# Statistics of 20 RMSNorm tiles: squares summed on GpSimd before one matmul, and weight casts on four DMA chains

## The reference

```python
def rmsnorm(x, g):
    x32 = x.astype(jnp.float32)
    y = x32 * lax.rsqrt(jnp.mean(x32 * x32, axis=-1, keepdims=True) + NORM_EPS)
    return y.astype(x.dtype) * g

u = modulate(rmsnorm(h, ffn1_norm[l]), sh1, sc1)
h = h + 0.5 * g1 * swiglu(u, ffn1_w_gate[l], ffn1_w_up[l], ffn1_w_down[l])
u = modulate(rmsnorm(h, mix_norm[l]), sh2, sc2)
h = h + g2 * hybrid_mixer(u, ...)
u = modulate(rmsnorm(h, ffn2_norm[l]), sh3, sc3)
h = h + 0.5 * g3 * swiglu(u, ffn2_w_gate[l], ffn2_w_up[l], ffn2_w_down[l])
return rmsnorm(h, final_norm)
```

## Time and profile before

| | us |
|---|---|
| median of 3 runs | 3066.21 |
| lowest and highest run | 3059.49, 3182.67 |
| the profiled execution's own time | 3062.68 |
| span of its slowest core, core 0 | 3061.1 |
| spans of the eight cores | 3041.2 to 3061.1 |
| mean granted PE clock of the cores | 0.983 to 0.985 |
| PE busy, share of the span | 2843.8, 93% |
| DVE busy | 1402.7, 46% |
| ACT busy | 1255.3, 41% |
| POOL busy (nearly all of it the issue of DMAs) | 75.1, 2% |

### The profile page before, as it was taken

The page is one execution under the profiler, slowest core; times in us unless marked ns, Lnnn a source line. Parts: engine busy times, 40 slices in busy tenths (PEclk is TensorE's granted clock), DMA queues, the critical chain, the costliest instruction groups (busy, mean ns, idle before and its releaser), DMA issues.

```text
span 3061.1 us, 42691 instructions; the slowest of 8 cores (3041.2 to 3061.1 us)
## 1 busy us (share of the span) xinstructions
PE 2843.8 (93%) x16528; PEld 1355.0 (44%) x16528; DVE 1402.7 (46%) x2808; ACT 1255.3 (41%) x1751; POOL 75.1 (2%) x147
## 2 busy tenths in 40 slices
PE   3999988999899999999978999999999999999998
PEld 1344433444454444544434445544454444444443
DVE  2555215445465445344445545654535444532532
ACT  2421105335434456454235453555755624322311
POOL 1000000000000000000000000000000000000000
PEclk9999999999999999999989999999999999999999
DMA  9678985476924934552793334334245368436446
GB/s 212 116 146 160 201 217 170 125 213 129 205 81 111 180 124 99 121 155 104 234 281 117 97 104 125 111 116 144 75 135 154 119 234 281 138 110 200 165 121 223
DMA packets 144138, 470.76 MB, mean 154 GB/s; under 512 B 17376, under 2 KB 21216, under 8 KB 129760
## 3 DMA queue, kind: packets, MB, share of 16 engines
q1 hardware_dynamic: 127600, 399.80, 41.2%
q0 software_dynamic: 16336, 68.23, 15.0%
HBM read 452.83 MB, written 100.66 MB: 181 GB/s over the span
## 4 chain that ended last, share of the span: by engine, by line
PE 75%; DMA 12%; ACT 5%; DVE 5%; SPq 1%; issue 1%; POOL 0%; ACTq 0%; DVEq 0%; POOLq 0%
PE psall L127 75%; ACT pt L127 3%; DMA hst<-xL 2%; DMA h<-hst 2%; DMA h<-qk 2%; DMA wf<-sdn 2%; SPq L127 1%; DMA wf<-wgu 1%; DMA wf<-w_ada 1%; ACT mu L127 1%; DMA qk<-h 1%; ACT L127 1%; DVE accsb L127 1%; DVE qk L127 1%; DVE mu L127 1%
## 5 line engine op out<-in xcount | busy, mean ns | idle before, releaser
L127 PE MATMUL psall<-uf,wf 128*128 128x512 bf16 x4224 | 1036.7, 384 | 39.7 <-DMA wf<-wgu 13.2
L127 ACT ACTIVATE pt<-psall 128x1024 bf16<-128x1024 f32 (+3 forms) x520 | 452.8, 872 | 458.4 <-PE psall L127 456.9
L127 PEld LDWEIGHTS psall<-uf,wf 128*128 128x128 bf16 x4224 | 399.9, 99 | 472.2 <-issue 36.7
L127 PE MATMUL psall<-actf,wf 128*128 128x512 bf16 x2112 | 514.4, 385 | 16.6 <-DMA wf<-sdn 16.6
L127 ACT ACTIVATE ftf<-psall 128x512 f32<-128x512 f32 x352 | 210.0, 597 | 658.3 <-PE psall L127 638.4
L127 DVE SCALAR_TENSOR_TENSOR ftf<-ftf,psall 128x512 f32<-128x512 f32 x352 | 241.1, 685 | 443.6 <-ACT ftf L127 412.5
L127 PE MATMUL psall<-mu,wm 128*128 128x512 bf16 (+2 forms) x1312 | 328.9, 381 | 13.7 <-ACT mu L127 9.6
L127 PE MATMUL psall<-mixb,wf 128*128 128x512 bf16 x1408 | 323.0, 384 | 9.0 <-ACT mixb L127 6.7
L127 PEld LDWEIGHTS psall<-actf,wf 128*128 128x128 bf16 x2112 | 200.0, 99 | 226.0 <-issue 18.7
L127 DVE SCALAR_TENSOR_TENSOR hst<-psall,SC,hst 128x512 f32<-128x512 f32 x120 | 90.0, 750 | 434.5 <-PE psall L127 260.4
L127 DVE TENSOR_TENSOR actf<-ftf,psall 128x512 bf16<-128x512 f32 x264 | 180.9, 685 | 195.2 <-PE psall L127 192.8
(11 more groups left out here) (113 smaller groups left out, 1993.6 us busy)
## 6 DMA issues: line engine op xcount, KB each, us to landing
wf<-sgu SPq DMA_DIRECT2D x242, 512.0 KB, 4.1
wf<-sdn SPq DMA_DIRECT2D x192, 352.0 KB, 4.2
h<-hst SPq DMA_DIRECT2D x120, 256.0 KB, 4.5
xt<-h SPq DMA_DIRECT2D x30, 1024.0 KB, 7.2
wm<-w_ada POOLq DMA_DIRECT2D x32, 512.0 KB, 11.0
hst<-xL SPq DMA_DIRECT2D x64, 256.0 KB, 7.4
qk<-h SPq DMA_DIRECT2D x16, 1024.0 KB, 6.6
h<-qk SPq DMA_DIRECT2D x16, 1024.0 KB, 9.6
```

The source lines that it names most:

```text
L127: ins = getattr(eng, o.fn[0])(**o.fn[1])
```

## The change

`pooled_stats` is new. It squares the eight pieces on ACT as before, but sums the squares on POOL: the first two into the float32 tile that later holds the reciprocal root (`rsf0`), the next ones onto it, and the last sum is written as bfloat16 into the buffer of the last square. Two empty steps follow, and then one matmul with the ones matrix. The PSUM bank is taken after that and not before. It applies to norms with the tag "XT" and a source and to `final_gen`; all other norms keep `square_stats`. The squares are still bfloat16. The casts of the FFN2 weights go round four resources and four semaphores instead of two.

```diff
+        def pooled_stats(pcs, sqr, acc, accR, out):
+
+            first = None
+            for k, (ap, res) in enumerate(pcs):
+                sq = square(ap, res, sqr)
+                if k == 0:
+                    first = sq
+                elif k == 1:
+                    I("pool", "tensor_tensor", r=[first[1], sq[1]], w=[accR], out=acc[:], in0=first[0][:], in1=sq[0][:], op=ALU.add)
+                elif k < len(pcs) - 1:
+                    I("pool", "tensor_tensor", r=[accR, sq[1]], w=[accR], out=acc[:], in0=acc[:], in1=sq[0][:], op=ALU.add)
+                else:
+                    I("pool", "tensor_tensor", r=[accR, sq[1]], w=[sq[1]], out=sq[0][:], in0=acc[:], in1=sq[0][:], op=ALU.add)
+                    out.append(sq)
+                yield
+            yield
+            yield
...
@@ norm_gen
+            rt, rtR = rs
+            total = []
+            if tag == "XT" and src is not None:
+                for _ in pooled_stats(pcs, sqr, rt, rtR, total):
+                    yield 1
             while not banks.free:
                 yield None
             bank = banks.take()
-            for _ in square_stats(pcs, sqr, bank, split):
-                yield 1
-            rt, rtR = rs
+            if total:
+                stat_mm(bank, total[0], 0, 1)
+            else:
+                for _ in square_stats(pcs, sqr, bank, split):
+                    yield 1
             rstd(bank, D, rt, rtR)
...
@@ final_gen
+            rt, rtR = rsF.next()
+            total = []
+            for _ in pooled_stats(XTP, btF, rt, rtR, total):
+                yield 1
             while not psF.free:
                 yield None
             bank = psF.take()
-            for _ in square_stats(XTP, btF, bank):
-                yield 1
-            rt, rtR = rsF.next()
+            stat_mm(bank, total[0], 0, 1)
             rstd(bank, D, rt, rtR)
...
-        convR = [Res("conv0"), Res("conv1")]
+        convR = [Res(f"conv{i}") for i in range(4)]
...
-                i = len(conv) % 2
+                i = len(conv) % 4
```

## The result

| | before | after |
|---|---|---|
| median, us | 3065.68 (8 runs) | 3083.27 (8 runs) |
| lowest and highest run | 3059.49, 3349.96 | 3078.97, 3094.76 |
| the profiled execution's own time | 3062.68 | 3082.51 |
| spans of the eight cores | 3041.2 to 3061.1 | 3058.1 to 3081.0 |
| mean granted PE clock of the cores | 0.983 to 0.985 | 0.975 to 0.979 |

The ratio is 1.007 (95% interval 1.0054 to 1.0087): within 2%, but slower by more than the measurement is uncertain.

What follows compares the result with a forecast made beforehand. PE's matmul count was taken as the bound, at the end and nearly so elsewhere. 3062.7 − 15.1 + 24.2 − 14.1 − 5 + 1 = 3053.7, plus 3.5 from profiled execution to median, gives 3057 us; range 3030 to 3092.

Steps and rivals of the forecast that it cites:

- all of it path: Ten dense tiles: 70 matmuls fewer at 0.216 us each shorten the kernel by their full 15.1 us.
- Add and pace: POOL's 140 new adds: 1.24 us each, one every 1.32 us with the gap between dependent adds.
- Quick adds: Rival, chance 0.18: POOL adds take 0.69 us, dense stall is 3.0 us instead of 24.2, time 3035 us.
- slow adds: Rival, chance 0.17: slower POOL adds lengthen PE's dense waits; at 2.0 us an add, stall 69 us and time 3102 us.
- Dense stall: Ten dense tiles: PE waits at the one matmul for the seventh add, 24.2 us in all, against 15.1 us saved.
- Costing it at nothing: Dense tiles: three square buffers hold ACT 6.5 us behind POOL's adds, counted as no loss of time.
- an add of 1.32 us keeps up, and the stall is 0 in all ten: Ten mixed tiles: steps lie 3 to 4 us apart, so PE never waits for adds; 14.1 us of matmuls gained.
- if the mixed stretches do not shorten: Sign named beforehand that the forecast is wrong: stretches where mixer and FFN interleave get no shorter.
- locks: Rival, chance 0.05: POOL and DVE exclude each other, 17 us of DVE delay in mixed stretches, time 3074 us.
- 5 us gained of the 9.5: FFN2 casts held back by adds: PE waits near 424 and 806 us shrink by 5 us, range 0 to 9.5.
- bursts of casts: Rival, chance 0.08: four casts at once delay weight loads at three places by some 5 us each, time 3077 us.
- The four chains themselves I cost at nothing: FFN2 casts on four chains instead of two: no cost, since the longest cast wait is 20.9 us.

Runs made afterwards that it cites:

- e5: The kernel after without POOL adds and without seven of eight squares, casts on two chains; ratio to the kernel before 0.994.
- e3: The kernel after with the one matmul five steps later in dense tiles; ratio to the kernel before 0.9995.
- e9: e6 with Ln of a pooled tile waiting only for the matmul, no longer for POOL as well; ratio to the kernel before 0.9913.
- e6: e3 with each FFN2 cast also waiting for the last PE instruction written before it (paced casts); ratio to the kernel before 0.9936.
- e14: e9 with the two mixed tiles at 1512 and 2157 us left on eight matmuls; ratio to the kernel before 0.9857, median 3021.59 us.
- e7: The kernel before with paced FFN2 casts and nothing else; ratio to the kernel before 0.9933.
- e11: e6 with every POOL add replaced by a memset of the same tile with the same waits; one run, 3069.86 us.
- e10: The kernel before with the casts on four chains and nothing else; ratio to the kernel before 1.0083.
- e1: The kernel after with only the ten dense tiles pooled, four chains of casts; ratio to the kernel before 1.0088.
- e2: The kernel after with only the ten mixed tiles pooled, four chains of casts; ratio to the kernel before 1.0014.
- e13: The kernel after with the casts on two chains as before; ratio to the kernel before 1.0036.

## Why the prediction was wrong

**Matmuls: count and pitch right, "all of it path" not quite.** 140 fewer, 0.216 us each. e5 gets 10.9 of 12.1 us from eight mixed tiles, e3 11.0 and e9 12.1 of the 15.1 from the ten dense ones. The 3 to 4 us that are missing in the dense stretches may have come out in the rest of the kernel, which gives 7.5 us in e3; that is not shown.

**Add and pace: right.** 1.30 us for 1.32. *Quick adds* and *slow adds* are both out.

**Dense stall: the wait about right, a term left out.** Forecast +9.1 us net, measured +20.8. PE's waits for POOL are 30.1 us as a mean over the cores (28.2 to 32.2). In order of the tiles they are 2.9, 10.6, 4.1, 0, 2.8, 2.2, 0, 2.8, 2.2 and 2.4 us, where the forecast had 2.2, 2.0, 3.8, 1.2, 2.9, 2.5, 1.2, 2.9, 2.5 and 3.0. The 10.6 us are not the adds alone. The seven adds take 8.9 us here, and they could not begin earlier, because the squares of this tile wait for its load (after, core 4):

```profile
346.98 1.67 ACT L127 ACTIVATE btf<-xt 128x512 bf16<-128x512 f32 x3 [22.97 <-DMA xt<-xL]
```

In this stretch PE waits 6.4 us before as well, for DVE and ACT, and 5.4 us in e3, so only about 5 of the 10.6 are new. That leaves about 25 us of new wait for the 24.2 of the forecast. The agreement of the sums is in part luck, since two tiles without a wait make up for the one with more. The step that failed in the dense tiles is that the sum ended with the wait: it had no term for the 1.2 GHz level behind it, 7 to 9 us. With the about 4 us of matmuls above, that is the 11.7 us between +9.1 and +20.8.

ACT, held by the three buffers, waits 14.7 us for POOL in the dense tiles (mean over the cores), where the prediction read 6.5. Costing it at nothing was right all the same: in e5 no add holds ACT, and its dense tiles gain no more than those of e3 (8.1 us against 11.0).

**Mixed tiles: the step that failed.** The prediction said "an add of 1.32 us keeps up, and the stall is 0 in all ten". Keep up it does, and PE never waits for POOL there; but a stall of 0 was read as a gain of 14.1, and in nine tiles the kernel loses 5.2 us where e5 gains 15.2. The prediction's own sign, "if the mixed stretches do not shorten", came. The 20.4 us between them, by differences of the table:
- after to e6, 3.2 us: casts held to their steps (e3, with the late matmul alone, gives nothing here: +6.7);
- e6 to e9, 4.8 us: the second wait, which puts the table load behind the matmul;
- e9 to e5, 12.4 us, of which 11.8 in two tiles: at 2157 us (+2.8 against −1.3) and at 1512 us (+3.4 against −4.3). The seven others differ by 0.6 us (−9.0 and −9.6): there pooling does give nearly what was forecast.

The tile at 2157 us shows its cause. The load of `w_ukv` comes (after, core 4) behind an add, itself held by its square. By the order of PE's own instructions it is issued 4.5 us later than before, in every core, and PE waits for it, 3.1 to 5.1 us by core, where before it does not wait:

```profile
2179.12 1.15 POOL L127 TENSOR_TENSOR rsf<-rsf,btf 128x512 f32<-128x512 f32 x1 [1.45 <-ACT btf L127]
2180.22 0.57 POOL L127 DMA_DIRECT2D wm<-w_ukv  x1
```

```profile
2186.84 1.03 PE L127 MATMUL psall<-mu,wm 128*64 128x512 bf16 x2 [5.06 <-DMA wm<-w_ukv]
```

With that tile as before (e14) the wait is 0.1 us. The prediction looked at one such load, w_in at 1513 us, found 53 us of cover, and went no further. At this tile, 1512 us, it asked only whether w_in itself comes too late, and it does not. But the adds also change how the four w_in loads are spaced. Before, they are issued 4 to 7 us apart; after (core 0), behind the third add, one and then three at once:

```profile
1522.06 0.57 POOL L127 DMA_DIRECT2D wm<-w_in  x1
1523.76 1.73 POOL L127 DMA_DIRECT2D wm<-w_in  x3 [1.13 <-DVE qk L127]
```

In the versions with this bunch PE waits longer for the loads of the down projection (`wf` from `sdn`) between 1490 and 1560 us: 14.5 us in the kernel after, 13.8 in e6 and 14.1 in e9, against 10.2 before, 10.1 in e5 and 9.8 in e14 (means over the cores). That fits the loss of this tile, and e14 takes both away, but no run spaces the loads out and keeps the adds, so it is not shown. A gain there has yet another source: e7, with no pooling, gains 4.0 us at this place by pacing alone.

Collisions with DVE are at most 1.2 us (e6 to e11, the latter one execution) for the 1 us forecast, so *locks* is out as a price, though the mechanism is there.

**Casts: a third place was missed.** "5 us gained of the 9.5": both gains came (9.6 and 4.5 us), and a third place, 612 us, took 14.1 back: net zero. The prediction held the casts "behind the adds of the tile whose last square is at 636.08" and gave their release there no price; the adds of that tile end at 619.4 us (core 4), and the three casts start there. The *bursts of casts* rival (0.08) had this mechanism, three casts at once beside a load, but put the delay on weight loads by 5 us each; it was one residual tile, and PE's wait for it 14.05 us in core 4. "The four chains themselves I cost at nothing" was wrong: 13.4 us alone (e10), 5.3 us within the change.

**Sum.** From −9.0 us forecast (without the 3.5 us between execution and median) to +18.8 are 27.8 us. Dense tiles: +11.7 (from +9.1 to +20.8). Nine mixed tiles: +17.0 (from nine tenths of −14.1 + 1, −11.8, to +5.2). Casts with the tenth tile: +7.1 (from −6.3 to +0.8, the four stretches from 400 to 1075 us). The rest of the kernel: −8.0, which no term of the sum holds. The terms that failed are thus the dense wait without its clock, the mixed gain, and the casts without their release. The 8.0 us of the rest are spread (2.8 between 130 and 335 us, 3.3 between 2440 and 2530) and come with the dense tiles' pooling (e1 −6.5, e2 −0.8); their cause was not looked for.

## What to carry to other kernels

To move work from a full engine to an idle one, place its consumer by the idle engine's pace: here five steps made the difference between +20.8 and −11.0 us in the same tiles. Add to a new wait of a few microseconds on PE the clock behind it, about 1 us a wait here, and look at every instruction that stands behind the new work in its engine's queue: loads get later, and background transfers that it happened to hold back are let go in a bunch. A forecast of a wait is also only as good as the start of the work before it: here one tile's squares began when its load had landed. Background transfers deserve a brake of their own: one dependency per cast gave 0.9933 without any other change.

## What was not expected of the hardware

- POOL starts dependent adds every 1.30 us for a duration of 1.15 us: 0.15 us between two, against the 0.05 us that the chain shows before. A memset of the same tile takes 525 ns, less than half an add:

```profile
L127 POOL MEMSET rsf<- 128x512 f32 x120 | 63.0, 525 | 1735.0 <-ACT btf L127 1628.0 <-DVE hst L127 101.7
```

- POOL adds make single DVE instructions wait for up to 0.99 us: a SCALAR_TENSOR_TENSOR of 128x4 (0.16 us) takes 1.15, the TENSOR_SCALAR above (0.28 us) 1.20, and a TENSOR_TENSOR of 128x512 1.64 for 0.68. The Trainium skill (SBUF — State Buffer, Who interferes with whom) has VectorE and GpSimd take turns at a shared port for whole instructions; the trace agrees, since one whole add is 1.15 us. Beside memsets nine instructions per core still stretch, to at most 0.63 us, by 2.1 us in all.
- With four DRAM-to-DRAM casts at once a load of one weight unit is out for 36 to 48 us (e10, by core). Between 612 and 645 us PE waits for DVE and its residual tile 12.4 us with three casts at once (after), 8.6 us with two (e13) and 0.3 us with one at a time (e6).
- An instruction of ACT that needs a new table and has two waits starts its table load only when the first wait is over: at 1924.00 us in e6, behind the matmul of 1923.54; at 1916.48 in e9, beside that of 1916.57. The load takes 1.28 us.
